# Row-by-row last down products and ScalarE high parts at the layer boundary of a two-layer encoder kernel

## The reference

```python
for l in range(DEPTH):                                   # DEPTH = 2
    h = x @ w_in[l]
    xf, q, k, v, g_f, g_a = jnp.split(h, SPLITS, axis=-1)
    ...
    x = layer_norm(DEEPNORM_ALPHA * x + mixed @ w_out[l], ln1_g[l], ln1_b[l])
    y_p = peer_ffn(x, peer_w_query[l], peer_sub_keys[l], peer_u[l], peer_v[l])
    x = layer_norm(DEEPNORM_ALPHA * x + y_p, ln2_g[l], ln2_b[l])
```

## Time and profile before

| | us |
|---|---|
| median of 3 runs (lowest, highest) | 3707.68 (3707.22, 3708.95) |
| profiled execution, its own time | 3706.67 |
| span of the profiled execution | 3704.9 |
| TensorE busy | 3658.8 |
| VectorE busy | 2641.4 |
| GpSimd busy | 2528.8 |
| ScalarE busy | 1230.8 |

### The profile page before, as it was taken

The page is one execution under the profiler, slowest core; times in us unless marked ns, Lnnn a source line. Parts: engine busy times, 40 slices in busy tenths (PEclk is TensorE's granted clock), DMA queues, the critical chain, the costliest instruction groups (busy, mean ns, idle before and its releaser), DMA issues.

```text
span 3704.9 us, 54023 instructions
## 1 busy us (share of the span) xinstructions
PE 3658.8 (99%) x18264; PEld 3014.4 (81%) x18264; DVE 2641.4 (71%) x4575; ACT 1230.8 (33%) x1815; POOL 2528.8 (68%) x1118
## 2 busy tenths in 40 slices
PE   8999999999999999999999999999999999999998
PEld 7778888888888888888887788888888888888886
DVE  7545999995665655877675469989856565668776
ACT  1651134454344433111125412344544344431110
POOL 6445554337999999877764555543379999997775
PEclk9999999999999999999999999999999999999999
DMA  4122235785333333545321223368843323335542
GB/s 154 69 69 103 103 142 178 239 247 180 125 132 140 113 125 133 219 183 191 136 104 69 80 96 109 140 192 244 245 153 149 123 114 129 150 140 190 206 182 102
DMA packets 225663, 546.32 MB, mean 147 GB/s; under 512 B 9728, under 2 KB 141056, under 8 KB 177280
## 3 DMA queue, kind: packets, MB, share of 16 engines
q1 hardware_dynamic: 47968, 337.14, 25.0%
q10 hardware_dynamic: 177568, 207.52, 17.0%
HBM read 441.86 MB, written 102.76 MB: 147 GB/s over the span
## 4 chain that ended last, share of the span: by engine, by line
PE 94%; DVE 3%; POOL 1%; issue 1%; DMA 1%; ACT 0%; DVEq 0%; ACTq 0%; POOLq 0%
PE bank L1554 29%; PE bank L1555 29%; PE bank L1556 29%; PE bank L1883 2%; PE bank L1884 2%; POOL part_l L524 1%; PE bank L1680 1%; PE bank L1843 1%; PE bank L1668 1%; PE bank L1659 0%; DMA gate<-dense_gates 0%; PE bank L1660 0%; DVE stats L1016 0%; POOL part_h L536 0%; DVE X L1044 0%
## 5 line engine op out<-in xcount | busy, mean ns | idle before, releaser
L524 POOL TENSOR_TENSOR part_l<-landing,part_h 128x1024 fp32r<-128x1024 f32 x512 | 1343.6, 2629 | 534.2 <-ACT part_h L784 456.3
L1554 PE MATMUL bank<-XTh,part_h 128*128 128x512 f32 (+1 forms) x2688 | 1047.9, 390 | 7.1 <-ACT Gf L679 2.9
L1556 PE MATMUL bank<-XTh,part_l 128*128 128x512 f32 (+1 forms) x2688 | 1034.1, 385 | 0.0
L1555 PE MATMUL bank<-XTl,part_h 128*128 128x512 f32 (+1 forms) x2688 | 1034.0, 385 | 0.0
L536 POOL TENSOR_SCALAR part_h<-landing 128x1024 fp32r<-128x1024 f32 x268 | 352.5, 1315 | 529.7 <-PE bank L1556 403.8
L1554 PEld LDWEIGHTS bank<-XTh,part_h 128*128 128x128 f32 x2688 | 505.3, 188 | 107.3 <-ACT Gf L679 3.7
L1556 PEld LDWEIGHTS bank<-XTh,part_l 128*128 128x128 f32 x2688 | 505.1, 188 | 101.5
L1555 PEld LDWEIGHTS bank<-XTl,part_h 128*128 128x128 f32 x2688 | 505.7, 188 | 95.5
L570 POOL TENSOR_TENSOR part_l<-vraw,part_h 128x1024 fp32r<-128x1024 f32 x210 | 525.5, 2527 | 63.0 <-ACT part_h L910 63.0
L1554 PE MATMUL bank<-part_h,Wh 128*128 128x512 f32 x1024 | 398.7, 389 | 0.9 <-POOL part_l L524 0.9
L1555 PE MATMUL bank<-part_l,Wh 128*128 128x512 f32 x1024 | 398.4, 389 | 0.0
(11 more groups left out here) (216 smaller groups left out, 6143.6 us busy)
## 6 DMA issues: line engine op xcount, KB each, us to landing
landing<-stream SPq DMA_DIRECT2D x256, 1024.0 KB, 4.8
dense_gates<-spill ACTq DMA_DIRECT2D x32, 2048.0 KB, 9.2
gate<-dense_gates ACTq DMA_DIRECT2D x62, 1024.0 KB, 4.8
vraw<-stream SPq DMA_DIRECT2D x60, 1024.0 KB, 6.5
early_acts<-early ACTq DMA_DIRECT2D x128, 256.0 KB, 2.3
acts_in<-early_acts ACTq DMA_DIRECT2D x32, 1024.0 KB, 7.5
LNP<-ln ACTq DMA_DIRECT2D x4, 1024.0 KB, 4.8
X<-x SPq DMA_DIRECT2D x4, 512.0 KB, 7.3
```

The source lines that it names most:

```text
L524: nc.gpsimd.tensor_tensor(halves(part_l[s], h), halves(landing[s], h), halves(part_h[s], h).bitcast(F32), ALU.subtract).then_inc(split.sem, 1)
L1554: nc.tensor.matmul(dst, sth, mvh, start=first, stop=False)
L1555: nc.tensor.matmul(dst, sth, mvl, start=False, stop=False)
L1556: return nc.tensor.matmul(dst, stl, mvh, start=False, stop=last)
```

## The change

The order of the eight last products becomes row block by row block (`LAST_ORDER`); `layer_norm` takes a list of blocks and is called for each block alone in this place (elsewhere for pairs, as before), with one root on ScalarE for each; the turns of blocks 0 and 1 come ahead of the two products of block 3; and in the first layer ScalarE copies the high parts of the next layer's pieces 0 and 1, GpSimd only makes their low parts.

```diff
@@ -48,6 +48,7 @@
 
+LAST_ORDER = [(tb, n) for tb in range(4) for n in range(2)]
 BLOCK_ORDER = [(0, 0), (1, 0), (0, 1), (1, 1), (2, 0), (3, 0), (2, 1), (3, 1)]
@@ -271,8 +272,8 @@
         xt_low = tally("xt_low", TB, 4 * TB)
-        root_in = tally("root_in", 2, 6)
-        root_out = tally("root_out", 2, 6)
+        root_in = tally("root_in", 2, 8)
+        root_out = tally("root_out", 2, 8)
         xf_copied = tally("xf_copied", 0, GROUPS)
@@ -612,7 +613,11 @@
             with pool.Fori(1, DEPTH) as l:
-                split_round(l, 0, 0)
+                for s in range(LANDINGS):
+                    for h in range(2):
+                        pool.sem_inc(went_on, 1)
+                        pool.wait_ge(high_part.sem, high_part.at(l, 2 * s + h + 1))
+                        low_half(s, h)
                 pieces_of(l)
@@ -992,10 +997,18 @@
                     down_highs(EG - 2 + par, par, (used.sem, used.at(l, S_DOWN + 2 * (EG - 2 + par))), None)
-                root(root_in.at(l, 5), slice(0, 2))
+                for tb in range(2):
+                    root(root_in.at(l, 5 + tb), slice(tb, tb + 1))
                 with act.If_lt(act.to_reg(l), DEPTH - 1):
-                    xt_parts([0, 1], TURN_LOW, lambda n: xt_bank.at(l, 3 * TB + n))
-                root(root_in.at(l, 6), slice(2, 4))
+                    for tb in range(2):
+                        xt_parts([tb], TURN_LOW[2 * tb:2 * tb + 2], lambda n: xt_bank.at(l, 3 * TB + 2 * tb + n))
+                        act.wait_ge(landed[tb], l * (8 * NS) + (8 * NS + 16))
+                        act.wait_ge(used.sem, used.at(l, S_LAST + tb + 1))
+                        for h in range(2):
+                            w = slice(h * PIECE // 2, (h + 1) * PIECE // 2)
+                            nc.scalar.copy(part_h[tb][:, w], landing[tb][:, w]).then_inc(high_part.sem, 1)
+                for tb in (2, 3):
+                    root(root_in.at(l, 5 + tb), slice(tb, tb + 1))
 
@@ -1015,17 +1028,17 @@
 
-            def layer_norm(ch, pair, n_root, n_par, in_banks=False):
+            def layer_norm(ch, blocks, n_root, n_par, in_banks=False):
 
                 ch.wait()
-                cols = slice(2 * pair, 2 * pair + 2)
-                for tb in (2 * pair, 2 * pair + 1):
+                cols = slice(blocks[0], blocks[-1] + 1)
+                for tb in blocks:
                     ch.mark(nc.vector.bn_aggr(mv[:, tb, :], stats[:, tb, :, :].rearrange("p a b -> p (a b)")))
...
                 dve.wait_ge(ln_in.sem, n_par)
-                for tb in (2 * pair, 2 * pair + 1):
+                for tb in blocks:
                     if in_banks:
@@ -1059,7 +1072,7 @@
                     half_stats(pre, tb, 1)
-                layer_norm(pre, pair, pair + 1, 16)
+                layer_norm(pre, (2 * pair, 2 * pair + 1), pair + 1, 16)
                 if pair == 0:
@@ -1246,7 +1259,7 @@
                         half_stats(ch, tb, 1)
-                    layer_norm(ch, pair, root_out.at(l, 3 + pair), ln_in.at(l, 16))
+                    layer_norm(ch, (2 * pair, 2 * pair + 1), root_out.at(l, 3 + pair), ln_in.at(l, 16))
                     low_parts([2 * pair, 2 * pair + 1], [4, 5, 6, 7], lambda n: xt_high.at(l, TB + TB * pair + n),
@@ -1532,20 +1545,22 @@
                 dve.wait_ge(y_added.sem, y_added.at(l, 4 * (NG - SG - 1)))
-                for pair in range(2):
-                    for tb in (2 * pair, 2 * pair + 1):
-                        dve.wait_ge(*rows_ready(l, 1, tb, NS))
-                        for h in range(2):
-                            rows = bank[2 * tb + h][:]
-                            ins = nc.vector.tensor_tensor(rows, X[:, tb, h * S:(h + 1) * S], rows, ALU.add)
-                        ins.then_inc(y_resid.sem, 1)
-                        dve.wait_ge(y_resid.sem, y_resid.at(l, tb + 1))
-                        for h in range(2):
-                            half_stats(ch, tb, h, bank[2 * tb + h][:])
-                    layer_norm(ch, pair, root_out.at(l, 5 + pair), ln_in.at(l, 32), True)
-                    if pair == 0:
+                for tb in range(TB):
+                    dve.wait_ge(*rows_ready(l, 1, tb, NS))
+                    for h in range(2):
+                        rows = bank[2 * tb + h][:]
+                        ins = nc.vector.tensor_tensor(rows, X[:, tb, h * S:(h + 1) * S], rows, ALU.add)
+                    ins.then_inc(y_resid.sem, 1)
+                    dve.wait_ge(y_resid.sem, y_resid.at(l, tb + 1))
+                    for h in range(2):
+                        half_stats(ch, tb, h, bank[2 * tb + h][:])
+                    if tb == 2:
                         with dve.If_lt(dve.to_reg(l), DEPTH - 1):
-                            low_parts([0, 1], TURN_LOW, lambda n: xt_high.at(l, 3 * TB + n))
+                            low_parts([1], TURN_LOW[2:4], lambda n: xt_high.at(l, 3 * TB + 2 + n))
+                    layer_norm(ch, (tb,), root_out.at(l, 5 + tb), ln_in.at(l, 32), True)
+                    if tb == 1:
+                        with dve.If_lt(dve.to_reg(l), DEPTH - 1):
+                            low_parts([0], TURN_LOW[0:2], lambda n: xt_high.at(l, 3 * TB + n))
 
@@ -1975,19 +1990,17 @@
                 pe.wait_ge(w_low.sem, w_low.at(l, CG * (NG - SG)))
-                for tb, n in BLOCK_ORDER:
+                for tb, n in LAST_ORDER:
                     if tb == 2:
                         pe.wait_ge(y_added.sem, y_added.at(l, 4 * (NG - SG - 1)))
-                    if (tb, n) == BLOCK_ORDER[-1]:
+                    if tb == 3:
                         with pe.If_lt(pe.to_reg(l), DEPTH - 1):
-                            turn_x([0], TURN_LOW[0:2], lambda n: x_normed.at(l, TB + n))
+                            turn_x([n], TURN_LOW[2 * n:2 * n + 2], lambda n: x_normed.at(l, TB + n))
                     ins = weighed_rows(bank[2 * tb + n], Wh[1], Wl[1], S_LAST + n, n, tb)
...
                         ins.then_inc(rows_done.sem, 1)
-                with pe.If_lt(pe.to_reg(l), DEPTH - 1):
-                    turn_x([1], TURN_LOW[2:4], lambda n: x_normed.at(l, TB + n))
 
```

## The result

| us | before | changed |
|---|---|---|
| median (lowest, highest; runs) | 3708.07 (3707.22, 3709.38; 8) | 3718.97 (3718.31, 3720.97; 8) |
| profiled execution, its own time | 3706.67 | 3718.68 |
| span | 3704.9 | 3716.7 |

The ratio of the changed kernel to the one before is 1.0029, with a 95% interval of 1.0019 to 1.0038: 10.9 us slower, where +4.1 was forecast, and outside the range given. The spans differ by 11.8 us.

The account below looks back on a forecast made before the run. TensorE, busy 3658.8 of 3704.9 us, was taken as the bound, with VectorE last at the boundary and end. +1.4 and +2.7 gave +4.1 us: 3710.8 profiled, 3711.8 by the median; range 3709.0 to 3715.0.

Parts of the forecast that it names:

- Part 1: Eight last products: new order makes TensorE wait 3.3 us instead of 0.6, +2.7 per layer; VectorE's start stays at 1839.60.
- Part 2: VectorE's norms: four single chains of 1.45 us for two pairs of 1.55, +2.7 us per layer; boundary +1.4, tail +2.7.
- block 2 is normed at 1863.2: Boundary, VectorE: time for block 2 after a 0.4 us root wait; block 3 then at 1870.1, against 1868.65.
- Part 3: Boundary: ScalarE's high parts keep GpSimd's low parts in time; TensorE ends 1.1 us before VectorE's low part.
- the return of 1.76 us: Boundary: TensorE's return to the head of the layer loop after the products, q products from 1859.0.
- Rival A: Boundary: GpSimd's low parts take 3.23 us, come late, TensorE ends last; 3712.8, or 3715 with longer return; chance 0.17.
- Rival C: TensorE's clock falls to 1.2 GHz after the new stalls of 1.1 and 2.1 us; 3715.1 and more; chance 0.06.
- slower by over 0.2%: Whole kernel: more than 7.4 us slower, through the clock rival and the end of the late-low-parts rival; chance 0.08.
- +1.4: Boundary, VectorE: +2.7 for chains, +0.4 for the root's wait, -1.7 for the old wait; pair 1 at 1872.6.
- 2.7 in the tail: End of layer 2: same start, VectorE's single norms add +2.7 us, same last stretch to memory.

Follow-up runs that it names:

- experiment 5: Changed kernel with the eight last products and two turns back in the old order; 3715.90 us, ratio 1.0021.
- experiment 1: Changed kernel with a single block's last three small chain operations taking the root as per-partition scalar, not second input tensor; 3713.19 us, ratio 1.0016.
- experiment 2: Changed kernel plus 16 matmuls on old data before the turn of blocks 2 and 3, in both layers' passes; 3722.05 us.
- experiment 3: Changed kernel with the high parts of the next layer's first two pieces back on GpSimd, without ScalarE's four copies; 3716.38 us, ratio 1.0022.
- experiment 6: Kernel before with only the order of the eight products and the turns changed; 3719.25 us, ratio 1.0029.
- experiment 9: Changed kernel plus 16 matmuls on old data before the turn of blocks 2 and 3, in the second layer's pass alone; 3720.20 us, ratio 1.0031.
- experiment 10: Kernel before with GpSimd's last low half part of piece 1 made to wait for the second pair's reciprocal; 3710.75 us, ratio 1.0005.
- experiment 7: Kernel before with VectorE's low parts of block 1 moved behind the statistics of block 2; 3708.18 us, ratio 0.9999.
- experiment 4: Kernel before with only the high parts moved to ScalarE, piece by piece behind each turned block; 3708.80 us, ratio 1.0002.

## Why the prediction was wrong

**Part 1, the order.** Right: waits of 1.0 and 1.8 us where I had 1.1 and 2.1, block 0 at the same moment, nothing won and nothing lost by it directly (experiment 5). Not seen: the two stalls can bring the clock down. Six profiled kernels have them at both layers' ends (the changed one and experiments 1, 2, 3, 6 and 9), and in 4 of these 12 places the clock fell behind the second stall (layer 2 of the changed kernel and of experiments 3 and 9, the boundary of experiment 6) and block 0 came 0.6 to 1.1 us later. With the one stall of the old order it fell in none of 12.

**Part 2, the norms.** The lengths were right where GpSimd was idle: 1.45 us for block 1's chain, +2.8 us for the tail. The step that failed is "block 2 is normed at 1863.2", which took its chain at 1.45 us too. It took 6.4 with the root's wait, because lines 1024 and 1025 were each held for one of GpSimd's low parts. This is the term that was missing, put at nothing in the sum: +4.3 us, shown by taking the second input away (experiment 1) and by making the meeting in the kernel before (experiment 10). In the kernel before, the chain of the second pair began at 1861.5 and its root was used at 1862.4, after GpSimd's last low part, which ended at 1861.8. The distance was 0.6 us, and the trace of the kernel before has both rows:

```profile
1862.43 0.16 DVE L1010 SCALAR_TENSOR_TENSOR rs<-rs 128x2 f32<-128x2 f32 x1 [0.27 <-ACT rs L623]
```

**Part 3.** Right that TensorE would not end last. Wrong that ScalarE's copies save what the new order would else have cost: without them the kernel was 2.6 us faster (experiment 3), since the closer row of low parts lengthens the hold. The q products began at 1857.9, not at 1859.0, only 0.5 us late behind the eight products: the return of 1.76 us that I read from the earlier trace rows was not there. In experiment 7 the first low part of block 1 ends at about 1856.7 and the q products have begun by then, so the low part that the row of the kernel before names is not what they wait for:

```profile
1856.06 1.27 DVE L1052 TENSOR_TENSOR XTl<-bank,XTh 128x512 fp32r<-128x512 f32 x2
```

```profile
1856.54 0.49 PE L1557 MATMUL bank<-part_h,XTh 128*128 128x512 f32 x1 [1.42 <-issue]
```

In the kernel before, the changed one and experiment 7 they begin 4.1 to 4.4 us after block 1 is normed, whatever lies between; what takes these 4 us is open.

**Rival A** had the two engines meet but only looked at GpSimd as the one that waits. The section of the Trainium skill that I cited (SBUF — State Buffer, "SBUF: two separate sides") says that whichever starts first keeps the ports for its whole instruction and the other is blocked, and the low parts started first. I tested its rule on VectorE's large passes, which read a bank, and wrote that the operations of this stretch each have one input in a bank. That is not so for the small chain: lines 1023 to 1025 read two tensors from SBUF. By that rule experiments 1, 3 and 10 come out as measured. The held operation on two columns with one input (experiments 4, 6 and 7) fits what it says of operations in a 2-port mode; that the operation ran in one, no run here shows.

**Rival C** was the other part: the clock fell after pair 0, but in the 3.76 us of idle time that the holds made, not behind the stalls that I had in view. With matmuls in that idle time, or without the holds, it stayed at 1.00 (experiments 1, 2 and 9). It cost 2.4 us there. With 0.06 for all outcomes through the clock, and none for a hold, the chance of 0.08 for slower by over 0.2% was far too small.

The sum with the terms as measured: +1.4 and 4.3 at the boundary, 2.4 and 0.7 for the clock, 2.7 in the tail, 11.5 of the 11.8 in the span. Not tried was the change with single norms alone, old order and high parts on GpSimd; what each of the three parts adds is known only from the combinations above.

## What to carry to other kernels

A chain of tiny VectorE operations costs little until a GpSimd operation runs beside it; then each link can cost a whole GpSimd instruction. Before moving either, lay their rows side by side and look for two-input operations in SBUF, however small, and write them with a per-partition scalar operand where a single column allows it. When VectorE ends last and starts when it did, as here, another order of TensorE's results wins nothing, and the idle time that it opens on TensorE may be paid again in clock.

## What the runs showed of the hardware

- A 128x1 operation of 0.16 us with two SBUF inputs took up to 2.32 us when it began during a GpSimd operation, to that operation's end. A GpSimd operation with one input holds too (0.97, experiment 3). The same arithmetic with a per-partition scalar operand took 0.21 and was not held (experiment 1).
- An operation with one SBUF input was held with two columns (1.93, 0.57, 0.44 us) and not with one (0.15).
- TensorE's granted clock fell after 3.8 us of waiting, inside the turn that ended the wait, and the matmuls of the next 5 us ran at 1.2 GHz. With a wait of 2.5 us (experiment 5) it fell as well; in the kernel before, with waits up to 1.5 us here, it did not. The length of the wait does not settle it: after waits of 2.96 us at the same place of the code, the clock was 0.50 in experiment 4 and 1.00 in experiment 5, and two stalls of 1.0 and 1.8 us brought it down in 4 of 12 places.
